# Two-layer mixer trunk: the low part of every fourth weight tile is subtracted on GpSimd instead of VectorE

## The reference, cut to what matters

```
def _layer(x, mem, ...):
    (r_q, r_k, r_v, a_cq, a_ckv, a_kpe, l_x, l_v, l_o, l_i, l_f, c_q, z) = _split_cols(x @ w_in, IN_SPLITS)
    ret = _merge(_head_norm(_retention(r_q, r_k, r_v), ret_norm_g))
    mla = _merge(_mla(a_cq, a_ckv, a_kpe, ...))          # rmsnorm of a_cq and a_ckv, softmax attention
    mls = ...                                            # causal conv, silu, mLSTM, head norm
    memo = _merge(_mem_attention(c_q, mem, w_mem_kv))    # softmax over (mem @ w_mem_kv)
    y = jnp.concatenate([ret, mla, mls, memo], axis=-1) * jax.nn.silu(z)
    y = y @ w_out
    return _layernorm(DEEPNORM_ALPHA * x + y, ln_g, ln_b)
for l in range(2): x = _layer(x, mem, ...)
```

## Time and profile before

| | us |
|---|---|
| median of three runs | 892.65 (892.63 to 893.07) |
| span of the profiled execution | 891.0 |
| outside the span (median less span) | 1.65 |
| PE busy | 884.9 (99%) |
| DVE busy | 661.6 (74%) |
| ACT busy | 490.7 (55%) |
| POOL busy | 18.0 (2%) |

### The profile page before, as it was taken

How to read it: one execution, slowest core, us unless ns; L and a number is a source line. 1 busy time by engine, 2 the same in 40 slices (tenths; PEclk the granted TensorE clock), 3 DMA queues, 4 the chain that set the end, 5 groups by cost and what they waited for, 6 DMA issues and landing times.

```text
span 891.0 us, 13209 instructions
## 1 busy us (share of the span) xinstructions
PE 884.9 (99%) x4548; PEld 759.8 (85%) x4548; DVE 661.6 (74%) x1312; ACT 490.7 (55%) x914; POOL 18.0 (2%) x18
## 2 busy tenths in 40 slices
PE   9999999999999999999999999999999999999997
PEld 8888998888888888888888889888888888888896
DVE  6869697877685677766668887968778747689865
ACT  6655775545555346544476556746354653575551
POOL 0000000000000000000000000000000001000001
PEclk9999999999999999999999999999999999999999
DMA  9796498447778687665665966875485865976932
GB/s 358 276 340 201 144 268 271 153 139 226 234 232 287 212 244 254 209 190 191 191 192 187 310 227 171 282 248 158 145 268 177 287 197 154 286 228 230 339 98 94
DMA packets 69650, 198.19 MB, mean 222 GB/s; under 512 B 8136, under 2 KB 21712, under 8 KB 68944
## 3 DMA queue, kind: packets, MB, share of 16 engines
q1 hardware_dynamic: 69008, 196.31, 67.8%
q10 hardware_dynamic: 576, 1.05, 0.4%
HBM read 182.38 MB, written 14.95 MB: 221 GB/s over the span
## 4 chain that ended last, share of the span: by engine, by line
PE 98%; issue 1%; DMA 0%; ACT 0%; POOL 0%; DVE 0%; POOLq 0%; ACTq 0%; DVEq 0%
PE acc L1335 24%; PE acc L1336 24%; PE acc L1339 24%; PE acc L1350 10%; PE acc L1356 5%; PE work L1102 1%; PE work L1101 1%; PE work L1100 1%; PE work L1240 1%; PE work L1239 1%; PE work L1095 1%; DMA B<-in_mem_t 0%; PE work L1262 0%; PE work L1251 0%; PE work L1179 0%
## 5 line engine op out<-in xcount | busy, mean ns | idle before, releaser
L1059 ACT ACTIVATE hi<-raw 128x512 fp32r<-128x512 f32 (+2 forms) x607 | 358.1, 605 | 317.1 <-PE acc L1339 255.5
L1422 DVE TENSOR_TENSOR lo<-raw,hi 128x512 fp32r<-128x512 f32 (+2 forms) x607 | 388.7, 657 | 174.5 <-ACT hi L1059 165.4
L1335 PE MATMUL acc<-hi,xx 128*128 128x512 f32 (+2 forms) x768 | 285.9, 375 | 0.0
L1336 PE MATMUL acc<-hi,xx 128*128 128x512 f32 (+2 forms) x768 | 283.6, 372 | 0.0
L1339 PE MATMUL acc<-lo,xx 128*128 128x512 f32 (+2 forms) x768 | 223.0, 372 | 0.0
L1335 PEld LDWEIGHTS acc<-hi,xx 128*128 128x128 f32 x768 | 144.6, 188 | 23.6
L1336 PEld LDWEIGHTS acc<-hi,xx 128*128 128x128 f32 x768 | 144.7, 188 | 23.5
L1339 PEld LDWEIGHTS acc<-lo,xx 128*128 128x128 f32 x768 | 140.4, 188 | 24.6
L1350 PE MATMUL acc<-xx,hi 128*128 128x512 f32 x384 | 96.1, 392 | 0.0
L1350 PEld LDWEIGHTS acc<-xx,hi 128*128 128x128 f32 x384 | 69.3, 189 | 12.6
L1356 PEld LDWEIGHTS acc<-xx,lo 128*128 128x128 f32 x384 | 52.4, 190 | 3.7
(11 more groups left out here) (348 smaller groups left out, 972.7 us busy)
## 6 DMA issues: line engine op xcount, KB each, us to landing
raw<-in_w SPq DMA_DIRECT2D x263, 512.0 KB, 4.3
B<-turn SPq DMA_DIRECT2D x80, 128.0 KB, 4.5
raw<-in_w SPq DMA_DIRECT2D x26, 256.0 KB, 2.7
turn<-B SPq DMA_DIRECT2D x12, 512.0 KB, 5.8
raw<-in_w SPq DMA_DIRECT2D x16, 328.0 KB, 3.3
turn<-Y SPq DMA_DIRECT2D x8, 512.0 KB, 5.6
Y<-in_wuq SPq DMA_DIRECT2D x2, 1152.0 KB, 8.6
Y<-in_x_t SPq DMA_DIRECT2D x4, 512.0 KB, 8.7
```

Source lines behind the costliest of these rows:

```text
L1059: act.activation(place(l, t, hi), raw[:, s, (t % 2) * w:(t % 2 + 1) * w], ACT.Copy)\
L1335: pe.matmul(o, ah[:, q], hi[:, s, 0:w], start=k == 0, stop=False, skip_group_check=name == "memv")
L1336: pe.matmul(o, al[:, q], hi[:, s, 0:w], start=False, stop=False, skip_group_check=name == "memv")
L1422: dve.tensor_tensor(place(l, t, lo), raw[:, s, (t % 2) * w:(t % 2 + 1) * w], place(l, t, hi).bitcast(F32), ALU.subtract).then_inc(lo_done. ...
```

## The change

Tile t of a layer with t % 4 == 3 (76 tiles a layer, 152 in all) gets its low part from GpSimd, and no longer from DVE. GpSimd now runs a loop over these tiles; its roots stand at fixed places in that loop: the two RMS roots behind tiles 83 and 99, the cell's behind 139, retention's behind 203 and 211; the LayerNorm's root and `ln_shift` stay behind the layer's last tile (303), and so ahead of tile 3 of the next layer. GpSimd waits for each of its own instructions before it goes on. A tile done on GpSimd counts on a semaphore of its own, `lo_by_pool`; PE and SP ask the one or the other by the tile's number (`wait_lo`), and SP waits for both tiles of a pair.

```
+POOL_AT = {}
+for _s, *_step in [(83, "rms", 0), (99, "rms", 1), (139, "cell", 0), (203, "ret", 0), (211, "ret", 1)]:
+    _put(POOL_AT, _s, *_step)
...
+        lo_done, lo_by_pool = signal("lo_done", SLOTS - SLOTS // 4), signal("lo_by_pool", SLOTS // 4)
...
+            if t % 4 == 3:
+                eng.wait_ge(lo_by_pool.sem, lo_by_pool.at(l, t // 4))
+            else:
+                eng.wait_ge(lo_done.sem, lo_done.at(l, t - (t + 1) // 4))
...
+                        wait_lo(sp, l, 2 * m - 2 * RAW)
+                        wait_lo(sp, l, 2 * m + 1 - 2 * RAW)
...
+                for t in range(3, SLOTS, 4):
+                    s, w = (t // 2) % RAW, width(l, PLACE[t][0])
+                    pool.wait_ge(hi_done.sem, hi_done.at(l, t))
+                    pool.wait_ge(tile_used.sem, tile_used.at(l, t - RING))
+                    pool.tensor_tensor(place(l, t, lo), raw[:, s, (t % 2) * w:(t % 2 + 1) * w],
+                                       place(l, t, hi).bitcast(F32), ALU.subtract).then_inc(lo_by_pool.sem, 1)
+                    pool.wait_ge(lo_by_pool.sem, lo_by_pool.at(l, t // 4))
+                    for name, *args in POOL_AT.get(t, ()):
+                        steps[name](*args)
...
-                        pe.wait_ge(lo_done.sem, lo_done.at(l, t))
+                        wait_lo(pe, l, t)
...
-            take_lo(0, 3)
...
-                    if l < DEPTH - 1 or t < SLOT_AT[LAST]:
+                    if (l < DEPTH - 1 or t < SLOT_AT[LAST]) and t % 4 != 3:
                         take_lo(l, t)
```

More of the change, by code:

```diff
@@ L474, in build_trunk @@
         hi_done = signal("hi_done", SLOTS)
-        lo_done = signal("lo_done", SLOTS, before=2 * RAW)
+        lo_done, lo_by_pool = signal("lo_done", SLOTS - SLOTS // 4), signal("lo_by_pool", SLOTS // 4)
         tile_used = signal("tile_used", SLOTS, before=RING)
@@ L537, in build_trunk, with wait_lo @@
         dve_own, act_own = signal("dve_own", 0), signal("act_own", 0)
+        def wait_lo(eng, l, t):
+            if t < 0:
+                l, t = l - 1, t + SLOTS
+            if t % 4 == 3:
+                eng.wait_ge(lo_by_pool.sem, lo_by_pool.at(l, t // 4))
+            else:
+                eng.wait_ge(lo_done.sem, lo_done.at(l, t - (t + 1) // 4))
         def wait_turned(eng, l, name):
@@ L674, in _ @@
                     if l or m >= RAW:
-                        sp.wait_ge(lo_done.sem, lo_done.at(l, 2 * m + 1 - 2 * RAW))
+                        wait_lo(sp, l, 2 * m - 2 * RAW)
+                        wait_lo(sp, l, 2 * m + 1 - 2 * RAW)
                     at, w = pair_at(l, m)
@@ L787, in _, with rms_root, cell_root, ret_root @@
             for l in range(DEPTH):
-                for r in range(2):
+                def rms_root(r):
                     pool.wait_ge(var_done.sem, var_done.at(l, r))
                     root(rms[:, r, :], sumsq[:, r, :], NT).then_inc(rms_done.sem, 1)
-                pool.wait_ge(cell_var.sem, cell_var.at(l, 0))
-                root(rstd[:, :], stats[:, :, 0], 8).then_inc(cell_pow.sem, 1)
-                for r in range(2):
+                    pool.wait_ge(rms_done.sem, rms_done.at(l, r))
+                def cell_root(_):
+                    pool.wait_ge(cell_var.sem, cell_var.at(l, 0))
+                    root(rstd[:, :], stats[:, :, 0], 8).then_inc(cell_pow.sem, 1)
+                    pool.wait_ge(cell_pow.sem, cell_pow.at(l, 0))
+                def ret_root(r):
                     pool.wait_ge(ret_var.sem, ret_var.at(l, r))
                     root(rstd[:, 0:4], stats[:, 0:4, 0], 4).then_inc(ret_pow.sem, 1)
+                    pool.wait_ge(ret_pow.sem, ret_pow.at(l, r))
+                steps = {"rms": rms_root, "cell": cell_root, "ret": ret_root}
+                for t in range(3, SLOTS, 4):
[7 more added lines that the diff above has]
+                        steps[name](*args)
                 if l == DEPTH - 1:
@@ L805, in _ @@
                 pool.tensor_tensor(ln_shift[:, :], ln_nmu[:, :], ln_rstd[:, :], ALU.mult).then_inc(ln_done.sem, 1)
+                pool.wait_ge(ln_done.sem, ln_done.at(l, 0))
         @block.scalar
@@ L1320, in _ @@
                             else:
-                                pe.wait_ge(lo_done.sem, lo_done.at(0, 0))
+                                wait_lo(pe, 0, 0)
                             for i in range(NT):
@@ L1404, in _ @@
                 dve.sem_inc(bank_read[b].sem, 1)
-            dve.sem_inc(lo_done.sem, 2 * RAW)
             links = [0]
```

## The result

The changed kernel takes 901.18 us (901.0 to 902.09), the kernel before 892.86 in the same job. The ratio is 1.0096, with a 95% interval of 1.0084 to 1.0108: slower by 7.5 to 9.6 us. The direction was the forecast one, the size was not: 3.65 us were forecast, with an upper end at 899.5.

The account below looks back on a forecast made before the run. PE was taken to bound the kernel, so relieving DVE gains nothing. Stalls of 2.05 us (tile 3, layer two) and 1.6 us (tile 87, both layers) sum to 3.65, forecasting 896.3 us; range 894.0 to 899.5.

Parts of the forecast that it names:

- What bounds the kernel: PE, busy 884.9 of 891.0 us, never waits for a low part; relieving DVE gains nothing, lateness is paid in full.
- Cost of one subtraction: On GpSimd, 0.25 us fixed plus twice DVE's column cost: 1.3 us for 512 columns, 0.93 for 328, 0.78 for 256.
- The forecast's other estimate: From the Trainium skill's GpSimd figure, about 1.4 us for 512 columns, which would make the sum 4.0 us.
- Term 1: Tile 3 of layer two, behind LayerNorm root and `ln_shift` on GpSimd: PE waits 1.83 us plus 0.2 exposed load, 2.05.
- Term 2: Tile 87 of each layer, behind RMS root 0 on GpSimd: 0.60 us late, 0.8 with exposed load, 1.6 in all.
- rival 1: GpSimd's subtractions also hold DVE up, 0.8 us late at RMS root 0; 897.9 us, or 899 with another stretch; chance 0.27.
- What is hidden: Tile 103, tiles behind other roots, SP's later pair waits and GpSimd's self-waits add nothing; plain lead some 5 us.
- Its signs: DVE's subtractions over 688 ns in the mean or idle time before them, and a stall over 1 us at tile 87.
- Rivals 2 and 3: 2: short subtraction, stalls under 0.2%, 894.2 us, chance 0.14; 3: faster, PE secretly waiting for DVE, at most to 891, 0.03.
- Rival 4: GpSimd starved between DVE's two-input instructions, subtractions 2 us and more, stalls at several narrow-tile chunks; 901 us, chance 0.11.

Follow-up runs that it names:

- relief_only: Kernel before, DVE subtracting only the first column of 151 tiles with t % 4 == 3 and nobody the rest; 892.75 us, ratio 0.9999.
- first_column: Changed kernel with GpSimd's subtractions cut to their first column, all but tile 3 of the first layer; 893.46 us, ratio 1.0008.
- roomy: Changed kernel, GpSimd keeping only 82 of 152 tiles, around which low parts were 3 us or more early, DVE doing the others; 892.76 us, ratio 1.0001.
- changed_again: Changed kernel, unaltered, run once more in the job of the later experiments; 900.38 us, ratio 1.0086.
- idle_one_operand: Kernel before, with 49 needless GpSimd products with 1.0, reading one operand, beside it in the first layer; 893.92 us, ratio 1.0012.
- idle_two_inputs: Kernel before, with 49 needless GpSimd subtractions, reading two operands, beside it in the first layer; 898.57 us, ratio 1.0061.

## Why the prediction was wrong

**What bounds the kernel: right.** Relief of DVE is worth 0 (relief_only), and lateness is paid in full: the stalls add up to the difference of the spans.

**Cost of one subtraction: right.** 1.37 us against 1.3. Fixed part 0.25: one column took 254 ns in first_column. The forecast's other estimate, 1.4 us, comes as close; the sum that it gave for it, 4.0 us, doesn't follow, since 0.1 us more at tile 3 and some 0.05 at each tile 87 make 3.85.

**Term 1: right.** 1.85 us, against 2.05. GpSimd's next start came 0.08 us after the product, not 0.15, and the exposed load was worth 0.11, not 0.2.

**Term 2: too small.** 1.28 and 1.27 us against 0.8. The sentence that failed is "without tile 83 DVE would be there at nearly the same time". DVE came 0.67 us late, which rival 1 had priced at 0.8. Most of it is the subtraction of tile 84 beside GpSimd's of tile 83, 0.98 us instead of 0.49 (POOL, DVE):

```profile
112.37 0.89 POOL L822 TENSOR_TENSOR lo<-raw,hi 128x328 fp32r<-128x328 f32 x1 [3.44 <-ACT hi L1091]
112.63 0.98 DVE L1453 TENSOR_TENSOR lo<-raw,hi 128x328 fp32r<-128x328 f32 x1 [0.35 <-ACT hi L1091]
```

Both terms together measured 4.4 us against 3.65.

**"What is hidden": this step failed.** It put everything else at nothing, because the plain lead of some 5 us would cover it. The lead is there in plain stretches, and roomy shows that 3 us cover. But of the 607 low parts that L1422 made before, 144 were done less than 3 us ahead of PE's wish, the start of the tile's first matmul on `lo`. Tile 81 and tile 25 of the first layer, before (DVE and PE each; tile 25 is the first of its DVE row and done at 39.78):

```profile
108.82 0.50 DVE L1422 TENSOR_TENSOR lo<-raw,hi 128x328 fp32r<-128x328 f32 x1
109.70 0.46 PE L1339 MATMUL acc<-lo,xx 128*128 128x328 f32 x2
...
39.10 1.28 DVE L1422 TENSOR_TENSOR lo<-raw,hi 128x512 fp32r<-128x512 f32 x2
41.07 0.61 PE L1339 MATMUL acc<-lo,mm 128*128 128x512 f32 x2
```

The leads are 0.4 and 1.3 us, and at the stalls in `cq` and `akv` they were 1.9, 2.1 and 0.9 (tiles 53, 57 and 71), against 4.8 at the boundary, where the forecast had read its lead. What it put at nothing measured 3.55 us in the profiled execution (the rows of `memk`, `cq`, `akv`, both `aq` and `w_out`), and 4.5 in changed_again. Without it the time would have lain inside the range. The 0.45 at tile 111 come from a late DMA, which no term had. One row at the boundary was taken for the whole program; the lead should have been read tile by tile.

**The rivals.** Rival 1 is what happens. Beside a subtraction on GpSimd, DVE's instructions of 512 columns with two SBUF inputs end 0.55 us behind its end, where they take 0.69 alone. Its signs came true: 759 ns in the mean, over 1 us at tile 87, and DVE busy for 639 us where the forecast had named 560. It was ranked second, with 0.27, because a root of four columns did not slow DVE. That row had been called undecided by its own sentence, and idle_one_operand suggests why: if shut out is the time in which GpSimd reads, four columns are read at once. That reading was not tested against others. Rows 7 and 11, in which GpSimd stands behind DVE to 0.01 us, were the better witnesses. And its price covered one crowded stretch (5.25 us, or 6.4 with another), where the trace has five (`memk`, `cq`, `akv`, `aq`, `w_out`). Rivals 2 and 3 did not come about. Rival 4 had 901 us, which is the measured time, and stalls at several chunks, but its mechanism was another: GpSimd's mean of 1.37 us excludes a starved GpSimd. That its number was met is luck.

The Trainium skill's rule (SBUF — State Buffer, "SBUF: two separate sides"), that the pair is held for the whole instruction by whichever comes first, agrees with the subtractions: DVE's of 512 columns, 0.69 us long alone, ended 0.55 us behind GpSimd's end. With one operand the measurement differs: DVE's instruction ended 0.34 us before GpSimd's.

## What to carry to other kernels

Before moving work to an idle engine, look whether the busy one bounds anything: here its relief was worth 0 and could only cost. Read the lead of every consumer tile by tile in the crowded stretches, not at one plain place. And count an elementwise instruction on GpSimd with two SBUF operands as time taken from VectorE's two-operand instructions too: here 100 us of rows moved away made VectorE's busy time 22 us shorter. An edit's gain that is read from one execution can hold a stall that is there or not by 0.03 us; look in the trace whether the edit touches it.

## What the runs showed of the hardware

**What is shut out.** Of DVE's 512-column subtractions in the changed kernel 48 began within the run of one on GpSimd, and 41 of them got longer. Of the other seven six began in its last 0.1 us, and one 0.01 us behind its start; there GpSimd's took 1.84 us. No instruction that reads PSUM (`acc`, `work`) got longer (POOL, DVE):

```profile
660.05 1.82 POOL L822 TENSOR_TENSOR lo<-raw,hi 128x512 fp32r<-128x512 f32 x1 [3.14 <-ACT hi L1091]
...
661.22 0.68 DVE L1811 TENSOR_TENSOR tmp<-acc,sin 128x512 f32<-128x512 f32 x1
```

Nor did nine transposes and two statistics. But one with a single operand of two columns did, 1.10 us instead of 0.17:

```profile
255.60 1.29 POOL L822 TENSOR_TENSOR lo<-raw,hi 128x512 fp32r<-128x512 f32 x1 [6.78 <-ACT hi L1091]
255.82 1.10 DVE L1839 TENSOR_SCALAR nmax<-nmax 128x2 f32<-128x2 f32 x1
```

**GpSimd's product with a constant is slower than its difference of two tensors**, 1793 ns against 1326 to 1366 for 512 columns in the mean, and 1.49 us against 1.04 (idle_two_inputs) and 1.26 (the changed kernel) at least, though it has one operand instead of two, and it holds DVE up for less.

**A memset of 512 columns on GpSimd takes 0.53 us** and leaves DVE's subtractions alone (688 ns).
